# Both ends of a two-layer decoder kernel: the order of its first loads, first products and last stores

## The reference

```python
def rmsnorm(x, g):
    y = x * lax.rsqrt(jnp.mean(x * x, axis=-1, keepdims=True) + EPS)
    return y * g

for l in range(2):
    x = x + 0.5 * rmsnorm(swiglu(rmsnorm(x, ffn1_pre_g[l]), ...), ffn1_post_g[l])        # phase 0
    x = x + rmsnorm(hybrid_mixer(rmsnorm(x, mix_pre_g[l]), cos, sin, ...), mix_post_g[l]) # phase 1
    x = x + rmsnorm(memory_cross_attn(rmsnorm(x, xa_pre_g[l]), ...), xa_post_g[l])        # phase 2
    x = x + 0.5 * rmsnorm(swiglu(rmsnorm(x, ffn2_pre_g[l]), ...), ffn2_post_g[l])        # phase 3
```

## Time and profile before

| | |
|---|---|
| median of three executions | 1249.93 us (1248.46 to 1251.76) |
| the profiled execution: its time | 1250.62 us |
| its span, first to last instruction | 1248.8 us |
| PE busy in the span | 1214.5 us (97%) |
| DVE, ACT, POOL busy | 801.1, 670.1, 153.7 us |
| mean granted clock of PE | 0.989 of full |
| PE's share of the chain that ended last | 89% |
| HBM read | 217.93 MB, 175 GB/s over the span |

### The profile page before, as it was taken

How to read it: one execution, slowest core, us unless ns; L and a number is a source line. 1 busy time by engine, 2 the same in 40 slices (tenths; PEclk the granted TensorE clock), 3 DMA queues, 4 the chain that set the end, 5 groups by cost and what they waited for, 6 DMA issues and landing times.

```text
span 1248.8 us, 19448 instructions
## 1 busy us (share of the span) xinstructions
PE 1214.5 (97%) x6120; PEld 1017.2 (81%) x6120; DVE 801.1 (64%) x1214; ACT 670.1 (54%) x1117; POOL 153.7 (12%) x282
## 2 busy tenths in 40 slices
PE   7999999998999999999999999999899999999997
PEld 5888888777898888888888888877779988888886
DVE  6766546766756576665476665567667557767655
ACT  6655436644655466553466553456457546555444
POOL 1000003642210010000010000037322001000001
PEclk9999999989999999999999999998999999999999
DMA  8556564442563355565465565463345544555563
GB/s 332 199 172 217 182 212 164 135 135 106 183 201 129 123 191 194 176 211 192 157 204 194 174 211 191 158 214 103 102 169 163 168 159 135 203 175 195 180 213 130
DMA packets 32916, 220.06 MB, mean 176 GB/s; under 512 B 4272, under 2 KB 4528, under 8 KB 8768
## 3 DMA queue, kind: packets, MB, share of 16 engines
q1 hardware_dynamic: 32544, 218.98, 51.2%
q10 hardware_dynamic: 288, 0.02, 0.0%
HBM read 217.93 MB, written 1.05 MB: 175 GB/s over the span
## 4 chain that ended last, share of the span: by engine, by line
PE 89%; DVE 4%; issue 2%; POOL 2%; ACT 1%; DMA 1%; DVEq 0%; ACTq 0%; SPq 0%; POOLq 0%
PE acc L465 27%; PE acc L467 27%; PE acc L466 26%; PE tb L524 3%; DVE w_lo L1182 2%; PE mb L615 1%; PE acc L774 1%; PE mb L758 1%; DMA raw<-in_gu 1%; PE mb L711 1%; ACT w_hi L870 1%; DVE pg L1316 0%; POOL r_head L1679 0%; PE mb L713 0%; DVE xT_lo L1188 0%
## 5 line engine op out<-in xcount | busy, mean ns | idle before, releaser
L1182 DVE SCALAR_TENSOR_TENSOR w_lo<-raw,gains,w_hi 128x512 fp32r<-128x512 f32 x580 | 416.3, 779 | 46.5 <-ACT w_hi L870 45.4
L465 PE MATMUL acc<-w_hi,xT_hi 128*128 128x512 f32 x1024 | 411.3, 402 | 8.4 <-DVE w_lo L1563 4.0
L467 PE MATMUL acc<-w_hi,xT_lo 128*128 128x512 f32 x1024 | 402.7, 393 | 0.0
L466 PE MATMUL acc<-w_lo,xT_hi 128*128 128x512 f32 x1024 | 402.2, 393 | 0.0
L870 ACT ACTIVATE w_hi<-raw,gains 128x512 fp32r<-128x512 f32 x580 | 369.9, 714 | 40.4 <-PE acc L467 40.2
L465 PEld LDWEIGHTS acc<-w_hi,xT_hi 128*128 128x128 f32 x1024 | 194.4, 190 | 51.3 <-DVE xT_lo L1188 5.1
L467 PEld LDWEIGHTS acc<-w_hi,xT_lo 128*128 128x128 f32 x1024 | 194.1, 190 | 41.7
L466 PEld LDWEIGHTS acc<-w_lo,xT_hi 128*128 128x128 f32 x1024 | 194.6, 190 | 37.8
L1176 DVE TENSOR_TENSOR w_lo<-raw,w_hi 128x1024 fp32r<-128x1024 f32 x112 | 123.6, 1145 | 72.6 <-ACT w_hi L864 71.9
L935 ACT ACTIVATE th<-acc,r_half 128x256 f32<-128x256 f32 x88 | 41.7, 474 | 197.3 <-PE acc L467 196.9
L864 ACT ACTIVATE w_hi<-raw 128x1024 fp32r<-128x1024 f32 x112 | 105.4, 991 | 77.2 <-PE acc L467 77.2
(11 more groups left out here) (175 smaller groups left out, 1250.2 us busy)
## 6 DMA issues: line engine op xcount, KB each, us to landing
raw<-in_gu SPq DMA_DIRECT2D x92, 1024.0 KB, 5.2
raw<-in_down SPq DMA_DIRECT2D x32, 1024.0 KB, 5.0
raw<-in_in SPq DMA_DIRECT2D x24, 1024.0 KB, 5.1
raw<-in_kv SPq DMA_DIRECT2D x16, 1024.0 KB, 5.2
raw<-in_down SPq DMA_DIRECT2D x16, 768.0 KB, 4.1
raw<-in_out SPq DMA_DIRECT2D x8, 1024.0 KB, 5.1
raw<-in_q SPq DMA_DIRECT2D x8, 1024.0 KB, 5.2
raw<-in_o SPq DMA_DIRECT2D x8, 1024.0 KB, 5.1
```

What stands on the lines that cost most here:

```text
L465: pe.matmul(o, st_hi, mv_hi, start=first, stop=False)
L466: pe.matmul(o, st_hi, mv_lo, start=False, stop=False)
L467: return pe.matmul(o, st_lo, mv_hi, start=False, stop=last)
L1182: dve.scalar_tensor_tensor(w_lo[:, slot, k, :], raw[:, slot, k, :], gains[:, ds(g, 1)], w_hi[:, slot, k, :].bitcast(F32), ALU.mult, ALU.su ...
```

## The change

It edits the start, the end, and small products of the norms.

- x tile 0 and the gains are issued by ACT, ahead of positions and inverse frequencies. SP issues the identity, then chunk 0 in eight DMAs of 256 KB (rows of 2 KB instead of 8 KB), each with a semaphore of its own, then x tile 1, chunk 1 and the constants as before.
- DVE's argument steps become 16 steps on POOL (`trig_arguments`), between the arrivals of x tile 0 and x tile 1. POOL also copies the sine tables. ACT takes the sines after chunk 0 and the square of x.
- PE runs eight matmuls of a matrix of ones before x arrives and three after its transposes (`WARM`). Their results are not used.
- The split of the first half of the chunk after next moves from the end of `boundary` to the beginning of what follows, `ffn` or `mixer`. So the last one of the kernel is gone, and the first one, of chunk 1, which stood ahead of the loop and of DVE's wait for the constants, now stands in the loop, behind it.
- The pair of a feed-forward waits for the split of x by halves (`x_split`) instead of for the whole tile.
- `pre` makes only the products that the next phase uses; the factor 1/D of the means moves into the scale of ACT's squares, and `post` starts with the first of its two sums.
- The output is stored in four quarters of 256 KB.

```diff
+            sp.dma_start(ident[:, :], a["ident"]).then_inc(s_ident, 16)
+            for h in range(2):
+                src, nk = weight_src(0, h, 0)
+                for k in range(nk):
+                    sp.dma_start(raw[:, h, k, :], src[:, k * COL:(k + 1) * COL]).then_inc(s_piece[4 * h + k], 16)
             sp.dma_start(x[:, 1, :], a["x"][P:2 * P, :]).then_inc(s_x_in[1], 16)
             load(0, 1)
...
+                for n in range(2):
+
+                    sp.wait_ge(s_x, 4 + 16 * (LAYERS - 1) + 12 + 2 * t + n + 1)
+                    sp.dma_start(out[t * P:(t + 1) * P, n * COL:(n + 1) * COL],
+                                 x[:, t, n * COL:(n + 1) * COL]).then_inc(s_out, 16)
...
-            pe.wait_ge(s_first, 32)
+            pe.wait_ge(s_ones, 1)
+            for _ in range(WARM[0]):
+                pe.matmul(mb[0][:, 0:P], ones[:, :], ones[:, :], start=True, stop=True)
+            pe.wait_ge(s_ident, 16)
             x_transposes(0, 0, 0)
...
                 y_square(l, phase, q, 1, 1)
-                split_hi(l, ci + 2, 0)
 
             def ffn(l, f):
                 c0, q0, phase = C_FFN[f], Q_FFN[f], (0, 3)[f]
+                split_hi(l, c0 + 1, 0)
                 split_hi(l, c0 + 1, 1)
...
+            act.dma_start(x[:, 0, :], a["x"][0:P, :]).then_inc(s_x_in[0], 16)
+            act.dma_start(gains[:, :], a["gains"]).then_inc(s_gains, 16)
             act.dma_start(pos_i[:, :], a["positions"]).then_inc(s_pos, 16)
             act.dma_start(inv_f[:, :], a["inv_freq"]).then_inc(s_pos, 16)
...
             x_square(0, 0, 0)
-            split_hi(0, 1, 0)
+            act.wait_ge(s_setup, 16)
+            act.activation(sin_t[:, :, :], rest[3][:, :, :], ACT.Sin).then_inc(s_trig, 1)
+            act.activation(cos_t[:, :, :], carg[:, :, :], ACT.Sin).then_inc(s_trig, 1)
             with act.Fori(0, LAYERS) as l:
...
-            split_lo(0, 1, 0)
             dve.wait_ge(s_const, 16 * 5)
             with dve.Fori(0, LAYERS) as l:
...
+                if phase == 1:
+                    pool.tensor_scalar(r_8[:, c], r_pre[:, c], DK ** -0.5, 0.0, ALU.mult, ALU.add)
+                    pool.tensor_scalar(r_half[:, c], r_pre[:, c], 0.5, 0.0, ALU.mult, ALU.add).then_inc(s_rpre, 1)
+                    return
                 then(pool.tensor_scalar(r_half[:, c], r_pre[:, c], 0.5, 0.0, ALU.mult, ALU.add))
                 pool.tensor_tensor(c_half[:, c], r_half[:, c], r_pre[:, c], ALU.mult).then_inc(s_rpre, 1)
```

146 lines of the change are left out of this document (84 added, 62 removed).

## The result

The changed kernel takes 1256.97 us in the median of five runs (1255.48 to 1257.88), against 1249.93 us before: a ratio of 1.0059, with a 95% interval from 1.0048 to 1.0071. It is slower by 7.0 us. The forecast was 1253.4 us with a range up to 1255.5, so the loss is twice the 3.5 us that I forecast. The profiled execution took 1257.58 us, with a span of 1255.8 us, 7.0 more than before.

The account below looks back on a forecast made before the run. PE was taken as the bound from 11.07 us to the last matmul. Start +5.0, middle -0.2 and end -1.3 sum to +3.5 us on 1249.9, so 1253.4 us; range 1249.0 to 1255.5.

Parts of the forecast that it names:

- The start: From the kernel's beginning to the end of pass 1: costs 5.0 us, pass 1 ending at 30.5 instead of 25.5.
- Pass 1: Second matmul pass, on chunk 1: begins at 21.6 instead of 18.86, 2.7 us late, behind DVE's wait for the constants.
- The clock: PE in pass 1: after idling, matmuls run at the lower clock level for some 11 matmuls, costing 2.3 us.
- Pass 0: First matmul pass, on chunk 0: first matmul at about 8.6 instead of 11.07, gaining nothing by itself.
- My own terms, 6.5 and 12.4: ACT at the start: transposes over by 6.5, then 12.4 us of work, first split of chunk 1 at about 18.
- rival 2: Start: ACT late, not constants; each microsecond its first chunk 1 split starts after 20.1 is added; e.g. 1254.6; chance 0.07.
- the single figure: Start: the last of the five constants lands at 20.4 us, taken from one execution; 17.9 the earliest possible.
- The moved splits keep their place in the order everywhere but at the two ends: Middle of the kernel: moving the splits changes the order only at the two ends; no cost counted elsewhere.
- The end: After the last matmul: 1.3 us gained, bounds 0.9 and 1.7, from earlier update of x and smaller last store.
- the smaller store: End: last store of 256 KB instead of 512 KB saves 0.7 us of transfer.
- The middle: Boundaries between start and end: shorter POOL chains and waits by halves give 0.2 us, bounds 0 and 0.5.
- Rival 1: Start: clock stays low through pass 1, from a slow stretch of about 5.5 us on; sum +4.7, 1254.6; chance 0.2.

Follow-up runs that it names:

- a_fill18: Changed kernel with the layer loop written out on PE and 18 unread matmuls of ones in PE's gap behind pass 0; 1254.52 us.
- a_edge_back: Changed kernel with the next chunk's first-half split put back ahead of the loop and at the end of phase 3; 1247.80 us.
- a_written_out: Changed kernel with nothing moved, the loop over the layers written out on ScalarE and VectorE; 1250.47 us.
- a_dve_written: Changed kernel with the loop over the layers written out on VectorE alone; 1252.17 us.
- a_const_late: Changed kernel with VectorE's wait for the five constants moved from ahead of the loop into the mixer; 1255.88 us.
- b_quarters: Kernel before with only the output store changed, to four quarters; 1248.30 us, ratio 0.9988 to 1.0007.

## Why the prediction was wrong

**The start was right in its sum and nearly in its steps.** Pass 1 was to begin at 21.6 and began at 21.42; it was to end at 30.5 and ended at 30.58. The clock was put at 2.3 us, and a_fill18 shows 2.4. Three details were off. Pass 0 began at 9.5, not 8.6, hidden by the wait as I said. ACT was ready at 19.1, not 18. My own terms, 6.5 and 12.4, add up to 18.9; what held ACT was POOL, which got the frequencies at 8.4, not 6, and let it wait 1.8 us ahead of the sines. So moving the constants' wait alone gave only 1.3 us. By the page of the Trainium skill that the prediction names, ACT would have begun at about 22, an estimate; by rival 2's own rule that adds 1.9 us, not the 1.2 in the text. And the last constant landed between 19.4 and 21.2 us in the executions of the versions with these loads, with the clock falling or not behind a gap (in the two profiles of the moved splits it fell behind 2.72 us and held behind 1.94), so the single figure was luckier than its working.

**The step that failed is the sentence "The moved splits keep their place in the order everywhere but at the two ends".** In the order of instructions that is true. But between layer 0 and layer 1 the splits changed sides of a jump, and I counted that at nothing, without naming what hid the jump. It costs 4.6 us: 2.66 us of PE's gap, and most of the rest at the lower clock behind it (granted clock 0.66 from 640 to 645). a_edge_back, a_written_out and a_dve_written each show it, and a_const_late, where the clock held, has 3.4 us behind a gap of 3.02. The trace of before had a faint sign of it: a hole of 0.68 us on DVE before 634.16, put down to a w_hi of ACT that had long been there, at the one place where a long loop begins anew. The prediction doesn't look at that stretch, because PE has no gap in it.

The Trainium skill has a rule for this, which the prediction doesn't weigh. The page "Runtime: NRT & Kernel Launch", section "Instruction fetch mechanics", says that a taken branch to a target outside the instruction pages at hand stalls the engine until they are fetched. The trace agrees: 5.1 us on DVE and 2.8 on ACT at the end of a layer (branch record to next instruction), with four packets on the instruction queue that go with the jumps. At the end of the short loop inside a feed-forward block it is 0.22 us on DVE (62.65 to 62.87 in the kernel before).

**The end was off by half.** Of my 1.3 us the earlier update of x gave 0.75 (I had 0.55), and the smaller store gave 0.0 to 0.2 instead of 0.7. The term itself was nearly right for three stores in four, which landed 0.5 us sooner than those of 512 KB; the last one did not, and why is open. The dead split's removal gave nothing of its own in the changed kernel: a_edge_back still has it, and its span ends 3.1 us after the last write of x as well, since its last store took 2.6 us and landed no sooner than the split ended.

**The middle can't be read:** it is -0.3 us between the start and the end of layer 0, against -0.2, but the mixer of layer 0 lies in this stretch, and in the other versions of the changed kernel the same stretch comes out between -2.3 and +1 us. That it fits is luck. **The matmuls of ones** bring nothing, as said.

**The sum.** 5.1 + 4.6 - 0.3 - 0.6 = 8.8 us. The spans differ by 7.0, since the mixer of layer 1 is 1.5 us shorter and the stretch ahead of it 0.2. The profiled execution of before had the longest value there, and by the column above, where b_quarters has -3.4 with the stores alone, this is chance rather than the change. Of the three rivals none had this mechanism. Rival 1 came nearest, for a wrong reason: the clock behind the first gap stayed low for about 5.2 us (21.4 to 26.6), close to the 4.8 I took and short of the 5.5 at which that rival begins. On rival 2 the trace again has 1.28 us for the table load with the next activation right behind it (17.83 to 19.12), not the 2.66 us of the page of the Trainium skill named in the prediction.

## What to carry over

When work moves across the beginning or the end of a loop, don't ask only whether it keeps its place in the order: look at the timeline of each engine at the loop's jump, and at what is queued ahead of it. In a long loop that work is the cover of the jump (3.8 to 5.8 us on VectorE here), and with it moved behind, the engine comes back late and everything that waits for it pays, with the lower clock on top. A wait moved to its first user and a loop written out are cheap trials of both. Here, together with the sines behind the urgent splits, they turned a loss of 7 us into a gain of 4, and of 5 without the matmuls of ones. Of that gain 2.6 us came in the kernel before too when only its loop was written out, for a reason that is open.
